# Two-head attention weights turned into the score banks, with two breaks of the projection stream per slot

## The reference, cut to what matters

```python
z = einsum(qb, kb) * scale
log_beta = log_sigmoid(z)
log_rem = where(causal, log_sigmoid(-z), 0.0)
suffix = cumsum(log_rem, reverse=True) - log_rem
attn = where(causal, exp(log_beta + suffix), 0.0)
out = einsum(attn, vb)
```

## Time and profile before

| | us |
|---|---|
| median of 3 runs (lowest, highest) | 1038.86 (1036.72, 1040.06) |
| the profiled execution, its own time | 1035.96 |
| its span, first to last instruction | 1034.2 |
| PE busy | 964.4 (93%) |
| DVE busy | 604.3 (58%) |
| ACT busy | 457.7 (44%) |
| POOL busy | 172.3 (17%) |
| mean granted TensorE clock | 0.977 |

### The profile page before, as it was taken

One profiled execution on the slowest core, in us unless ns is written; L12 is line 12 of the kernel. 1 busy time (PEld: TensorE's weight loads), 2 busy tenths in 40 slices (PEclk: granted clock), 3 DMA queues, 4 the chain that ended last, 5 costly groups with the idle time before them and its releaser, 6 DMA issues.

```text
span 1034.2 us, 14258 instructions
## 1 busy us (share of the span) xinstructions
PE 964.4 (93%) x4981; PEld 760.3 (74%) x4981; DVE 604.3 (58%) x1108; ACT 457.7 (44%) x811; POOL 172.3 (17%) x144
## 2 busy tenths in 40 slices
PE   2399999899999899999999998999999999988995
PEld 2358777678777688777787776778878888866883
DVE  2854685565875566865657855642653333254766
ACT  1142556554565463665454565543743322242221
POOL 1100022231122230121420122320200000001220
PEclk9699999999999999999999999999999999999998
DMA  8703111011211102111012111105621211223222
GB/s 295 237 11 76 42 31 42 21 42 29 75 30 45 27 21 62 51 34 37 20 41 72 31 42 27 36 22 172 224 92 46 67 51 41 92 91 113 82 102 101
DMA packets 77485, 71.61 MB, mean 69 GB/s; under 512 B 4700, under 2 KB 66268, under 8 KB 77436
## 3 DMA queue, kind: packets, MB, share of 16 engines
q1 hardware_dynamic: 73116, 58.31, 19.5%
q0 software_dynamic: 2592, 8.52, 2.4%
q10 hardware_dynamic: 1728, 4.20, 1.0%
HBM read 62.49 MB, written 8.39 MB: 69 GB/s over the span
## 4 chain that ended last, share of the span: by engine, by line
PE 86%; DVE 4%; ACT 3%; issue 3%; DMA 2%; SPq 1%; POOL 0%; ACTq 0%; DVEq 0%; POOLq 0%
PE bank L613 45%; PE bank L593 9%; PE bank L594 8%; PE bank L595 8%; PE bank L728 3%; PE bank L712 3%; PE bank L697 2%; PE bank L682 1%; DMA x_rows<-in_x 1%; ACT rem L983 1%; DMA a_raw<-in_w_ada 1%; PE bank L699 1%; PE bank L698 1%; DVE a_acc L1294 1%; PE bank L755 1%
## 5 line engine op out<-in xcount | busy, mean ns | idle before, releaser
L613 PE MATMUL bank<-hH,wH 128*128 128x512 f32 x704 | 290.9, 413 | 0.7 <-DVE wL L1308 0.7
L613 PE MATMUL bank<-hH,wL 128*128 128x512 f32 x704 | 278.0, 395 | 0.0
L613 PE MATMUL bank<-hL,wH 128*128 128x512 f32 x704 | 277.0, 393 | 0.0
L552 POOL TENSOR_TENSOR ez<-ez,rem 128x512 f32<-128x512 f32 (+3 forms) x96 | 135.1, 1426 | 469.0 <-DVE rem L1469 469.0
L1308 DVE SCALAR_TENSOR_TENSOR wL<-w_raw,wH 128x512 fp32r<-128x512 f32 (+1 forms) x122 | 94.0, 772 | 142.2 <-ACT wH L902 140.9
L613 PEld LDWEIGHTS bank<-hH,wH 128*128 128x128 f32 x704 | 133.7, 190 | 36.0 <-issue 10.6
L613 PEld LDWEIGHTS bank<-hH,wL 128*128 128x128 f32 x704 | 133.0, 189 | 29.8
L613 PEld LDWEIGHTS bank<-hL,wH 128*128 128x128 f32 x704 | 134.0, 190 | 24.9 <-issue 1.0
L902 ACT ACTIVATE wH<-w_raw 128x512 fp32r<-128x512 f32 (+1 forms) x122 | 75.5, 620 | 106.1 <-PE bank L595 74.6
L1469 DVE TENSOR_TENSOR_SCAN rem<-rem,ones 128x512 f32<-128x512 f32 (+3 forms) x96 | 88.5, 964 | 32.8 <-ACT rem L987 32.8
L974 ACT ACTIVATE ez<-bank 128x512 f32<-128x512 f32 (+3 forms) x96 | 41.9, 489 | 54.3 <-PE bank L699 53.7
(11 more groups left out here) (236 smaller groups left out, 1478.4 us busy)
## 6 DMA issues: line engine op xcount, KB each, us to landing
w_raw<-in_w_in SPq DMA_DIRECT2D x104, 256.0 KB, 2.9
a_raw<-in_w_ada SPq DMA_DIRECT2D x16, 512.0 KB, 4.7
x_rows<-in_x SPq DMA_DIRECT2D x8, 512.0 KB, 7.1
raw<-in_w_ada POOLq DMA_DIRECT2D x8, 512.0 KB, 6.1
x_in<-in_x SPq DMA_DIRECT2D x8, 512.0 KB, 4.1
out_y<-res SPq DMA_DIRECT2D x8, 512.0 KB, 2.9
raw<-in_w_out SPq DMA_DIRECT2D x10, 256.0 KB, 4.2
ysb_scratch<-y_stage ACTq DMA_DIRECT2D x8, 256.0 KB, 3.0
```

The source lines that it names most:

```text
L552: g.tensor_tensor(e, e, r, ALU.mult).then_inc(a_done[h], 1)
L613: ins = t.matmul(proj_ps[half][:], w, a, start=(r == 0), stop=(r == JOB_MM // 2 - 1))
```

## The change

1. The transposes of the weights go into `z_ps[h]`, the bank from which the same head's scores have been read, and `at_ps` is gone. In slot `s` both heads of slot `s-1` are turned together; each waits until ACT has read this slot's scores (`ex_done`), and the scores of slot `s+1` wait until ACT has copied the turned weights out (`at_out`).
2. PE's slot has two stretches of projection matmuls (16 and 16, later 13 and 14) and two groups of other work. The first group is `mlstm_first`, `weighted_values` of slot `s-2`, `scores`; the second is both heads' `turn_weights`, `mlstm_second`, `mlstm_third`.
3. The transposes of `next_v` and the L784 matmuls move from ahead of slot 0 into slots 0 and 1. With them ACT's copy of v (`token_major`) moves to slot 0, DVE's `chunk_weights` to slot 1, ACT's exp of the decay weights to slot 2, and DVE's `mask_chunk_weights` from slot 0 to slot 3, between `conv_bound` and `conv_silu`.
4. The gate steps get a number of their own on each engine: the sum `z_sum` at 266 (slot 7), the Exp `z_exp` at 278 (end of slot 7), the product `z_mul` at 292 (slot 8), in place of 254, 254 and 262 in slot 7.
5. ACT copies both heads out one after the other, behind the middle part's tasks; on DVE `chunk_scores` goes ahead of `cap_odds`.

```diff
-        sizes = (10, 10, 12) if s < 3 else (9, 9, 9)
+        sizes = (8, 8, 16) if s < 3 else (7, 6, 14)
...
-    found = [(JOB_MM * 4 + 6, 2, "o_log", 0, 0), (JOB_MM * 5 + 6, 2, "z_log", 0, 0),
-             (JOB_MM * 5 + 14, 2, "z_exp", 0, 0), (JOB_MM * 5 + 22, 2, "z_mul", 0, 0)]
+    found = [(JOB_MM * 4 + 4, 2, "o_cap", 0, 0), (JOB_MM * 4 + 14, 2, "o_log", 0, 0),
+             (JOB_MM * 5 + 4, 2, "z_cap", 0, 0), (JOB_MM * 5 + 14, 2, "z_log", 0, 0),
+             (JOB_MM * 5 + 26, 2, "z_sum", 0, 0), (JOB_MM * 5 + 38, 2, "z_exp", 0, 0),
+             (JOB_MM * 6 + 4, 2, "z_mul", 0, 0)]
...
+            def turn_weights(i, s):
+
+                for h in range(2):
+                    if s + 1 < NS:
+                        pe.wait_ge(ex_done[h], i * NS + s + 2)
+                    pe.wait_ge(a_done[h], i * NS + s + 1)
+                    for b in range(n_keys(s) // P):
+                        ins = t.transpose(z_ps[h][:, b * P:(b + 1) * P], ez[s % 2][h][:, b * P:(b + 1) * P], ident[:])
+                    ins.then_inc(at_filled[h], 1)
...
+                project(i, 0, PRE)
                 for s in range(NS):
-                    a, b, c_, d = segs[s]
+                    start, _, middle, end = segs[s]
+                    mlstm_first(i, s)
+                    if s > 1:
+                        weighted_values(i, s - 2)
                     scores(i, s)
-                    project(i, a, b)
+                    project(i, start, middle)
                     if s > 0:
-                        turn_weights(i, s - 1, 0)
-                    mlstm_first(i, s)
-                    project(i, b, c_)
-                    if s > 0:
-                        turn_weights(i, s - 1, 1)
+                        turn_weights(i, s - 1)
                     mlstm_second(i, s)
                     mlstm_third(i, s)
-                    project(i, c_, d)
-                    if s > 0:
-                        weighted_values(i, s - 1)
+                    project(i, middle, end)
+                weighted_values(i, NS - 2)
...
                 if s == 0:
-                    mask_chunk_weights(i)
                     pair_gate(i)
                 if s == 1:
+                    chunk_weights(i)
                     conv_sum(i, 2)
...
                 if s == 3:
                     conv_bound(i, 1)
+                    mask_chunk_weights(i)
                     conv_silu(i, 1)
...
-                chunk_weights(i)
                 for s in range(NS):
                     p0, p1, p2, p3 = segs[s]
+                    place0(i, s)
                     cap_odds(i, s)
```

More of the change, by code:

```diff
@@ L143, in tail @@
     at = segments()[0][-1][-1]
-    third = (JOB_MM * NJ - at) // 3
-    return [at, at + third, at + 2 * third, JOB_MM * NJ]
+    return [at, at + (JOB_MM * NJ - at) // 2, JOB_MM * NJ]
 def events(lo, hi):
     n = NJ
-    found = [(JOB_MM * 4 + 6, 2, "o_log", 0, 0), (JOB_MM * 5 + 6, 2, "z_log", 0, 0),
-             (JOB_MM * 5 + 14, 2, "z_exp", 0, 0), (JOB_MM * 5 + 22, 2, "z_mul", 0, 0)]
+    found = [(JOB_MM * 4 + 4, 2, "o_cap", 0, 0), (JOB_MM * 4 + 14, 2, "o_log", 0, 0),
+             (JOB_MM * 5 + 4, 2, "z_cap", 0, 0), (JOB_MM * 5 + 14, 2, "z_log", 0, 0),
+             (JOB_MM * 5 + 26, 2, "z_sum", 0, 0), (JOB_MM * 5 + 38, 2, "z_exp", 0, 0),
+             (JOB_MM * 6 + 4, 2, "z_mul", 0, 0)]
     for j in range(n):
@@ L699, in scores @@
                     t.matmul(ps, qL[r, tt], kH[r, kk], start=False, stop=True).then_inc(z_done[h], 1)
-            def turn_weights(i, s, h):
-                if h == 0:
-                    if s > 0:
[L705 to L713, removed]
+            def turn_weights(i, s):
[6 more added lines that the diff above has]
+                    ins.then_inc(at_filled[h], 1)
             def weighted_values(i, s):
@@ L758, in mlstm_third @@
             def mlstm_third(i, s):
+                if s == 0:
+                    for n in range(2):
+                        pe.wait_ge(m_drained[n], m_count(n, i, F_V))
+                        if n == 0:
+                            pe.wait_ge(drained[1], job(i, -2) + 1)
+                        transposes(n, [next_v[:, cc * P:(cc + 1) * P] for cc in range(4 * n, 4 * n + 4)])
+                if s == 1:
+                    pe.wait_ge(h_cols, i + 1)
+                    for n in range(2):
+                        pe.wait_ge(m_drained[n], m_count(n, i, F_R))
+                        t.matmul(misc_ps[n][:], sel_cur[0:32, :], bm[0:32, halves(n)], start=True, stop=True)\
+                            .then_inc(m_filled[n], 1)
                 if s == 2:
@@ L773, in iteration @@
                 segs, _ = segments()
[L774 to L785, removed]
+                project(i, 0, PRE)
                 for s in range(NS):
-                    a, b, c_, d = segs[s]
+                    start, _, middle, end = segs[s]
+                    mlstm_first(i, s)
+                    if s > 1:
+                        weighted_values(i, s - 2)
                     scores(i, s)
-                    project(i, a, b)
+                    project(i, start, middle)
                     if s > 0:
-                        turn_weights(i, s - 1, 0)
-                    mlstm_first(i, s)
-                    project(i, b, c_)
-                    if s > 0:
-                        turn_weights(i, s - 1, 1)
+                        turn_weights(i, s - 1)
                     mlstm_second(i, s)
                     mlstm_third(i, s)
-                    project(i, c_, d)
-                    if s > 0:
-                        weighted_values(i, s - 1)
+                    project(i, middle, end)
+                weighted_values(i, NS - 2)
                 ends = tail()
                 project(i, ends[0], ends[1])
-                turn_weights(i, NS - 1, 0)
+                turn_weights(i, NS - 1)
                 project(i, ends[1], ends[2])
-                turn_weights(i, NS - 1, 1)
-                project(i, ends[2], ends[3])
                 weighted_values(i, NS - 1)
@@ L994, in turned @@
                     act.wait_ge(pv_done[h], i * NS + s)
-                a.activation(at_sb[h][:, 0:w], at_ps[:, 0:w], ACT.Copy).then_inc(at_out[h], 1)
+                a.activation(at_sb[h][:, 0:w], z_ps[h][:, 0:w], ACT.Copy).then_inc(at_out[h], 1)
             def store_y(i, tc):
@@ L1103, in place1 @@
                 if s == 0:
+                    token_major(i, F_V, v_tok)
+                if s == 2:
                     act.wait_ge(w_sum, i + 1)
@@ L1132, in iteration @@
                     remainders(i, s)
+                    tasks(i, p1, p2, last)
                     if s > 0:
                         turned(i, s - 1, 0)
-                    tasks(i, p1, p2, last)
+                        turned(i, s - 1, 1)
                     place1(i, s)
-                    if s > 0:
-                        turned(i, s - 1, 1)
                     place2(i, s)
@@ L1143, in iteration @@
                 turned(i, NS - 1, 0)
-                tasks(i, ends[1], ends[2], last)
                 turned(i, NS - 1, 1)
@@ L1149, in iteration @@
                 a.activation(small[:, 24:32], small[:, 24:32], ACT.Exp, scale=-0.5).then_inc(rstd_exp, 1)
-                tasks(i, ends[2], ends[3], last)
+                tasks(i, ends[1], ends[2], last)
                 store_y(i, 1)
@@ L1660, in iteration @@
                         conv_silu(i, 0)
-                    place0(i, s)
+                    if s == 5:
+                        gate_y(i, 0)
                     tasks(i, p0, p1, last)
```

16 lines of the change are left out of this document (7 added, 9 removed).

## The result

The changed kernel took 1042.58 us (median of 6 runs, 1040.68 to 1045.38) against 1037.8 us for the kernel before, measured beside it (6 runs, 1036.62 to 1040.06). The ratio is 1.0049 with a 95% interval of 1.0034 to 1.0064: slower by 3.5 to 6.6 us. The profiled executions have spans of 1034.2 us before and 1038.9 us now, 4.7 apart.

A forecast was written before the change was run, and what follows sets the result against it. PE, busy 93% of a 1034.2 us span, was taken to bound the kernel. Terms -22.4 + 11.6 + 4.5 + 7.6 + 0.8 = +2.1 us, on 1038.86, gave 1041.0 us; range 1031 to 1052.

The forecast's parts named there:

- the signs named: Slot 7's wait gone; PE idle 2.5 to 3.5 us at slot 4 (`m_q`), 1 to 2.5 at slot 9 (`m_num`).
- points 1 to 3: Slot 7's stall (13.0 us), the slow clock behind it (4.5) and small copy waits in slots 5 and 8 (3.6) disappear.
- point 4: Twelve fewer breaks of PE's projection stream per iteration, at 0.035 us each, save 1.3 us net.
- Rival C: A break of PE's projection stream costs 0.2 us, 9.6 us instead of 1.7: 1033 us; chance 0.08.
- point 5: Start of slot 4: PE waits 2.9 us for `conv_done`, four times, adding 11.6 us (10.8 to 14).
- The term of 0.2 us for the mask: Slot 4 wait: POOL beside DVE's mask lengthens the chain to `conv_done` by 0.2 us (0 to 0.8).
- point 7: Start of slot 9: `mlstm_first` waits 1.9 us for slot 8's `m_num`, adding 7.6 us in all.
- point 8: Slots 8 and 10 start within 0.1 us of their banks: 0.2 us an iteration, 0.8 us added.
- point 6: The clock falls behind three of four slot 4 waits, 1.5 us each, adding 4.5 us (0 to 6).
- Rival A: New waits at slots 4 and 9 stay short or keep the clock: 1029 or 1036.5 us; chance 0.19.
- rival D: Slot 7's stall is not removed, since ACT still waits for the sum: +17 us; chance 0.03.
- Rival B: DVE behind POOL delays starts: 3.7 us at slot 4, 2.9 at slot 9, clock falls; 1053 us; chance 0.2.

The follow-up runs named there:

- experiments 5 and 6: The kernel before with only the gate steps' new numbers: 1018.07 us; and with only each head's turned weights in its own score bank: 1021.59 us.
- kernel with both moves: The changed kernel with slot 4's `mlstm_first` moved to its second group and `z_mul` at 294 instead of 292: 1013.65 us, repeated at 1014.59 us.
- experiment 9: The changed kernel with the mask of the decay weights behind `conv_silu` instead of ahead of it: 1042.56 us.
- the kernel with the scores first: The changed kernel with `mlstm_first` behind the weights times v and the scores at every slot's start: 1024.43 us.

## Why the prediction was right, point by point

The predicted time, 1041.0 us, is 1.6 below the measured 1042.58, inside the range. The step against the kernel before was too small: +2.1 us, where 3.5 to 6.6 were measured. That the time came closer than the step is luck: it was counted from 1038.86, the median of three runs, and six gave 1037.8. The three-way chances put most on slower, but with only 0.40. Of the signs named, both stops came with the length and the releaser foretold; a low clock behind the slot 4 stop "in most iterations" came in two of four.

- *The slot 7 stall, its clock, and the small waits* (points 1 to 3, 13.0 + 4.5 + 3.6 = 21.1 us): right. They are gone from the trace. The numbers alone gave 20.4 us and left 1.3 of waits; numbers and banks together gave 23.4. That each of the two reasons named there is enough by itself, experiments 5 and 6 show, with the numbers of the caps and logs counted to the first.
- *The breaks* (point 4, 1.3 us): right in kind. 44 breaks cost 0.4 us and the whole new order gave 0.6, neither told from nothing. Rival C, at 0.2 us a break, fell. The kernel with both moves is 24.0 to 24.7 us faster than before, against 22.4 taken away in the sum.
- *`conv_done` at slot 4* (point 5, 2.9 us each, 11.6 in all): 3.0 each, 12.0 in all. The term of 0.2 us for the mask was wrong: it cost nothing (experiment 9). POOL did block it, for 1.1 us (2.30 against 1.22), but this fell into the 2.2 us in which DVE waited for ACT anyway, and the wait hangs on the slower of the two branches. The Trainium skill, "SBUF — State Buffer", section "SBUF: two separate sides", has a VectorE instruction with two SBUF inputs fully blocked while a GpSimd one that reads SBUF holds the port pair that they share. The trace agrees: the mask ended 1.09 us behind POOL's product. The 3.7 us that I had worked out with this rule for PE's wait did not come.
- *The chunk's banks at slot 9* (point 7, 1.9 us each, 7.6 in all): 1.8 to 1.9, 7.3 in all, by the chain named, with the product at 2.03 and the split at 1.45, both with POOL beside them.
- *Slots 8 and 10* (point 8, 0.8 us): no such wait is in the list.
- *The clock* (point 6, 4.5 us): the term that was too small, and most of the difference in the result. The size of one fall, 1.5 us, was right, and the count was not. The sum gave a fall to three of the four slot 4 stops and none to slot 9, which stood in rival B only; in the changed kernel's trace the clock fell behind two stops of slot 4 and three of slot 9. Five at 1.5 are 7.5, 3.0 more than the sum had. With 0.4 more for point 5, 0.3 less for point 7 and 0.8 less for point 8 that is 2.3 of the 2.6 us by which the profiled executions (4.7 apart) exceed the forecast step. What was taken away then comes out as 12.0 + 7.3 + 7.5 - 4.7 = 22.1, near the sum's 22.4. The clock also falls outside the loop, differently from one execution to the next (last section), so each of these balances is good to some 2 us.
- *Rival A* (short waits or a clock that stays) and *rival D* (the old stall stays) fell. *Rival B* named the right place for the missing part, slot 9, where it had the clock fall half the time; its falls at every stop of slot 4, its wait of 3.7 us there and its 2.9 in slot 9 did not come.

## What to carry to other kernels

Moving a waiting instruction to the head of a group moves everything behind it on that engine under its wait: before merging two groups, take the end of the chain that each of their semaphores hangs on, and compare it with the new place. Here one matmul that had been 0.8 us behind its input was put some 4 us of PE work ahead of that place, and it came to wait 3.0 us; with a second, shorter wait of the same kind that gave back all of a 24 us gain. Moving three matmuls in one slot and one number in a table brought it back. A place in a shared queue counts like a buffer: giving the gate steps numbers of their own, so that ACT's Exp waited 2.1 us for its sum and not 14.4, was worth 20 us alone, and a bank for each head 17 alone; together they gave 23.

## What the runs showed of the hardware that was not expected

- A stop of 1.8 us can cost the clock and one of 3.0 us can leave it up. In the changed kernel the granted clock fell to 0.50 behind three of four stops of 1.8 us and behind two of four of 3.0 us, though the program is the same in each iteration. In the kernel with the scores first it fell behind three of four stops of 1.7 us. The prediction had gone by the length of the stop alone; the length does not decide it here. What does was not settled.
- The runs of one kernel differ by their clock. For the changed kernel the mean granted clock was 0.975 in the run of 1040.68 us, 0.974 in those of 1041.77, 1042.45 and 1042.71, 0.972 at 1044.44 and 0.971 at 1045.38; 0.004 of 1040 us is 4.2 us, close to the 4.7 between the first and the last. But stops in the loop are not needed for this: the kernel with both moves, which has none there, lay within 1011.63 to 1015.58 us over its ten runs. Its two profiled executions (1015.51 and 1011.63 us) differ at a stop of 2.37 us behind the loop that both have. This is the clock behind it, first in experiment 3's trace, then in its repetition's:

```profile
905.00:911.00 6.00, 6.00 (x20) 4.71 (x20) 5.64 (x9) 2.24 (x5) 0.00 (x0) 0.72 0.44 145
...
902.50:908.50 6.00, 6.00 (x27) 4.81 (x27) 5.67 (x9) 2.38 (x5) 0.00 (x0) 1.00 0.46 145
```

So how much of the changed kernel's spread its eight stops make is not shown.
